# Last two chunks of a gated delta rule begin in rounds 1 and 2 instead of round 4, with the wait for one weight's split moved to their fourth step

## The reference

```python
# half 1: gated delta rule, 4 heads of 128, one scan forward and one backward
kk = einsum('bnhik,bnhjk->bnhij', k, k)
a_low = where(strict, kk * decay * beta[..., :, None], 0.0)
uw = triangular_solve(a_low + eye(C), rhs, left_side=True, lower=True, unit_diagonal=True)
def step(S, xs):                      # chunk after chunk
    v_new = u_i - einsum('bhck,bhkv->bhcv', w_i, S)
    o_i = einsum('bhck,bhkv->bhcv', q_i, S) + einsum('bhij,bhjv->bhiv', qk_i, v_new)
    S = S * gl_i[..., None, None] + einsum('bhck,bhcv->bhkv', k_i, v_new)
# half 2: attention with 8 query heads and 2 key heads of 64, rotated by row and column
o_at = axial_gqa_group(aq, ak, av, q_norm, k_norm)
mix = concatenate([o_dn, o_at], axis=-1) @ w_out
```

## Time and profile before

| | us |
|---|---|
| median of three runs | 1135.56 |
| the profiled execution's own time | 1134.65 |
| its span | 1132.9 |
| busy: PE / DVE / ACT / POOL | 1080.2 / 750.3 / 608.4 / 93.3 |
| delta stage on PE, first gates product to last `o` product | 799.14 to 915.85 |

### The profile page before, as it was taken

One profiled execution on the slowest core, in us unless ns is written; L12 is line 12 of the kernel. 1 busy time (PEld: TensorE's weight loads), 2 busy tenths in 40 slices (PEclk: granted clock), 3 DMA queues, 4 the chain that ended last, 5 costly groups with the idle time before them and its releaser, 6 DMA issues.

```text
span 1132.9 us, 19901 instructions
## 1 busy us (share of the span) xinstructions
PE 1080.2 (95%) x8119; PEld 959.5 (85%) x8119; DVE 750.3 (66%) x1254; ACT 608.4 (54%) x1098; POOL 93.3 (8%) x120
## 2 busy tenths in 40 slices
PE   6999998999999999999999999999679999999998
PEld 3989567989899899889899988999568878998986
DVE  1686887899997866567755447786575756444443
ACT  2544755554354556657445465547764536555453
POOL 0012671000000000000000000022420000000000
PEclk9999999999999999999999999999788999999999
DMA  9998116799998455433855652260000145555540
GB/s 371 408 400 339 39 38 260 269 347 370 347 354 301 149 186 187 144 135 144 339 195 187 229 177 106 75 259 2 1 2 21 40 153 200 186 186 186 186 149 38
DMA packets 33562, 218.27 MB, mean 193 GB/s; under 512 B 4528, under 2 KB 5296, under 8 KB 8896
## 3 DMA queue, kind: packets, MB, share of 16 engines
q1 hardware_dynamic: 33472, 217.00, 51.8%
HBM read 215.93 MB, written 1.05 MB: 192 GB/s over the span
## 4 chain that ended last, share of the span: by engine, by line
PE 79%; DVE 8%; ACT 7%; DMA 2%; issue 2%; POOL 1%; DVEq 0%; SPq 0%; ACTq 0%; POOLq 0%
PE bank L527 21%; PE bank L529 21%; PE bank L528 21%; ACT high L515 2%; DVE low L521 2%; DMA ring<-ada_halves 2%; PE bank L567 1%; PE bank L2485 1%; PE bank L644 1%; DVE y_tmp L1608 1%; PE bank L1150 1%; DVE stats L1610 1%; DVE y_tmp L1597 1%; PE bank L2774 1%; DMA ring<-raw_ksv 1%
## 5 line engine op out<-in xcount | busy, mean ns | idle before, releaser
L521 DVE TENSOR_TENSOR low<-ring,high 128x2048 fp32r<-128x2048 f32 (+1 forms) x139 | 317.4, 2286 | 234.9 <-ACT high L515 234.4
L515 ACT ACTIVATE high<-ring 128x2048 fp32r<-128x2048 f32 (+1 forms) x139 | 264.7, 1906 | 246.1 <-PE bank L529 171.0
L527 PE MATMUL bank<-act_high,high 128*128 128x256 f32 (+1 forms) x1072 | 308.5, 288 | 0.0
L529 PE MATMUL bank<-act_high,low 128*128 128x256 f32 (+1 forms) x1072 | 303.6, 283 | 0.0
L528 PE MATMUL bank<-act_low,high 128*128 128x256 f32 (+1 forms) x1072 | 303.5, 283 | 0.0
L527 PE MATMUL bank<-high,act_high 128*128 128x512 f32 (+1 forms) x632 | 233.3, 369 | 3.1 <-DVE act_low L3080 1.8
L529 PE MATMUL bank<-high,act_low 128*128 128x512 f32 (+1 forms) x632 | 230.8, 365 | 0.0
L528 PE MATMUL bank<-low,act_high 128*128 128x512 f32 (+1 forms) x632 | 230.6, 365 | 0.0
L527 PEld LDWEIGHTS bank<-act_high,high 128*128 128x128 f32 x1072 | 204.8, 191 | 4.7 <-issue 2.6
L528 PEld LDWEIGHTS bank<-act_low,high 128*128 128x128 f32 x1072 | 205.0, 191 | 2.4 <-issue 1.4
L529 PEld LDWEIGHTS bank<-act_high,low 128*128 128x128 f32 x1072 | 204.8, 191 | 0.0
(11 more groups left out here) (514 smaller groups left out, 1339.6 us busy)
## 6 DMA issues: line engine op xcount, KB each, us to landing
ring<-chunks SPq DMA_DIRECT2D x138, 1024.0 KB, 5.1
ring<-ada_halves SPq DMA_DIRECT2D x38, 1024.0 KB, 6.6
o_land<-ada_halves SPq DMA_DIRECT2D x6, 1024.0 KB, 11.4
ring<-raw_cmp SPq DMA_DIRECT2D x4, 1024.0 KB, 11.2
x_tok<-ada_halves SPq DMA_DIRECT2D x3, 1024.0 KB, 14.9
gate_rows<-ada_b SPq DMA_DIRECT2D x4, 512.0 KB, 9.7
bias<-bias_by_distance SPq DMA_DIRECT2D x1, 2048.0 KB, 12.9
ln_rows<-ln_g SPq DMA_DIRECT2D x4, 512.0 KB, 6.0
```

What stands on the lines that cost most here:

```text
L515: e.activation(weights(c)[0], in_ring(("w", c)), ACT.Copy).then_inc(*act.up("high", c))
L521: e.tensor_tensor(low, in_ring(("w", c)), high.bitcast(F32), ALU.subtract).then_inc(*vec.up("low", c))
L527: e.matmul(out_, ah, bh, start=start, stop=False)
L529: return e.matmul(out_, al, bh, start=False, stop=stop)
```

## The change

The last two chunks begin in rounds 1 and 2. What stood in their way is rearranged: `qdec` leaves the slots of OUT2 and OUT2+1 for a free place; the wait for the `low` of OUT2+1 goes from step 1 on PE to step 4 on DVE, and to the zeroing of `xT` on POOL, and step 1 waits for IN2+10 alone. Their scaled rows (`bv`, `bek`, which share a buffer with the meta chunk) are written one level later.

```diff
-                      **{... for i, n in enumerate(("x", "xT", "bek", "qdec"))},
+                      **{... for i, n in enumerate(("x", "xT", "bek"))},
                       "bv": mem.take(f"d{d}_bv_last", 4, P, at=after_cols + 8 * L2 + d * 512),
+                      "qdec": mem.take(f"d{d}_qdec_last", 4, P, at=(late_at + 6 * P + (2 * JOIN + 1) * HALF, after + 336 + D)[d]),
...
             elif not first:
-                e.wait_ge(*low_made(OUT2 + 1))
+                e.wait_ge(*low_made(IN2 + 10))
...
-            rows_level = 1 if first else 3
+            rows_level = 1 if first else 4
...
             e.wait_ge(*vec.at("a", k))
+            if real and not first:
+                e.wait_ge(*low_made(OUT2 + 1))
...
-        CHUNKS = (((0, 2), 0), ((1, 2), 0), ((0, 0), 0), ((1, 1), 0), ((0, 1), 4), ((1, 0), 4))
+        CHUNKS = (((0, 2), 0), ((1, 2), 0), ((0, 0), 0), ((1, 1), 0), ((0, 1), 1), ((1, 0), 2))
...
             e.wait_ge(*act.at("w", (d, t)))
+            if d != t:
+                e.wait_ge(*low_made(OUT2 + 1))
```

More of the change, by code:

```diff
@@ L2008, in program @@
         last_bufs = [{**{n: mem.take(f"d{d}_{n}_last", 4, P, at=early_at[d] + i * 512) for i, n in enumerate(("a", "aT", "w"))},
-                      **{n: mem.take(f"d{d}_{n}_last", 4, P, at=late_bufs[d] + i * 512) for i, n in enumerate(("x", "xT", "bek", "qdec"))},
+                      **{n: mem.take(f"d{d}_{n}_last", 4, P, at=late_bufs[d] + i * 512) for i, n in enumerate(("x", "xT", "bek"))},
                       "bv": mem.take(f"d{d}_bv_last", 4, P, at=after_cols + 8 * L2 + d * 512),
+                      "qdec": mem.take(f"d{d}_qdec_last", 4, P, at=(late_at + 6 * P + (2 * JOIN + 1) * HALF, after + 336 + D)[d]),
                       "qk": first_bufs[d]["qk_last"]} for d in range(2)]
```

## The result

The changed kernel takes 1137.81 us (median of 20 runs, 1132.62 to 1141.15), the kernel before beside it 1134.62 us (20 runs, 1130.49 to 1138.06). The ratio is 1.0024, with a 95% interval of 1.0013 to 1.0035: slower, by about 3 us. The profiled execution of the changed kernel, though, took 1133.5 us, less than the 1134.65 us of the one of before. It is one of the fastest of its twenty. That has to be explained first.

What follows compares the result with a forecast made beforehand. PE was taken as the bound, busy 95%, with 13.7 us idle from 804 to 850 us. The front's 3.1 us plus 1.65 us at the end made 4.8 us slower: 1139.8 us, range 1131 to 1146.

Steps and rivals of the forecast that it cites:

- the sum's main term: First part of the delta stage: round 8 ends 6.0 us late, minus 2.9 us of steps ahead, net 3.1 us late.
- the right ones: Signs: DVE round 3 at 820 to 822 us, ACT idle 6 us, logits 7 to 10 late, PE full, two holes.
- signs of being wrong: Logits before 836 us, PE idle under 13.7 us before it is full, or step 2 making ACT wait at no cost.
- the second rival: Delta stage: lateness equals the 2.9 us of steps ahead, only 1.65 us at the end remain; 1136.3 us, chance 0.17.
- The holes at the end: PE idle 0.75 us before the o product of (1, 0) and 0.9 us before the last values, together 1.65 us.
- The queue of DVE: Round 2: moved steps make DVE begin round 3 at about 821.1 us instead of 816.48, 4.6 us late.
- Round 3 on DVE: Its former 8.4 us, slow instruction included, plus 3.2 us of moved work, ending at 832.7 us.
- ACT's wait: ACT idle 6 us or more before the qdec exponential of (1, 0), behind DVE; first logits 8.9 us late.
- From the logits to the end of round 8: On PE, 19.9 us before the change shrink by 2.9 us of waits to 17.0 us; round 8 ends at 856.4.
- The clock: Rival: one more half-clock stretch on PE costs some 2.8 us, 1142.5 us, or one fewer, 1137.0; chance 0.15.
- The filled idle time: Rival: moved steps fill PE's idle time in the first part; -4.4 us, 1130.3 us, at most -6.7; chance 0.23.

Runs made afterwards that it cites:

- e5: Changed kernel plus 13 idle products, whose results nobody reads, in places where PE waits; ratio 0.9999 to the kernel before.
- e11: Kernel before plus 16 idle products in its two long PE waits; ratio 0.9976 to the kernel before.
- e9: Changed kernel with only (0, 1) early, in round 1, and (1, 0) in round 4 as before; 1130.2 us, ratio 0.9970 to the kernel before.
- e10: Changed kernel with only (1, 0) early, in round 2, and (0, 1) in round 4 as before; ratio 0.9995 to the kernel before.
- e4: Changed kernel with the last chunks' two step 2 exponentials written one round later on ACT; ratio 1.0003 to the kernel before.
- e2: Changed kernel without its new starting rounds, keeping the moved waits, new qdec place and later rows; ratio 0.9999 to the kernel before.
- e12: Kernel e9 plus 14 idle products in PE's waits; ratio 0.9953 to the kernel before, six executions.
- e3: Changed kernel plus 28 idle products at four places where PE waits in the first part; ratio 1.0032 to the kernel before.

## Why the prediction came out, and where its steps were wrong

The sign, the size (forecast 4.8 us by the sum, measured 3.2 us) and the range held. But the sum's main term was not what made the kernel slower, so that the number came out is in large part luck: a front that was to lose 3.1 us did not, and a clock that was given 0.15 cost about as much.

The prediction's own signs say so. Three of the right ones came (ACT idle for 6.69 us, PE full from 850 us on, two holes of 0.89 and 0.77 us at the end); DVE began round 3 just before its 820 us; the logits were 5.2 us late and not 7 to 10. And both signs of being wrong that have a number came: the logits at 835.73, before 836 us, and PE idle for 10.0 us from 804 to 850, less than 13.7. ACT reached the meta keys at 834.83, which was the condition of the second rival, *only the end counts*. Of the three it tells best what the profiled order does; the rest of the loss is the clock's.

- **The holes at the end**, 1.65 us forecast: 0.89 and 0.77 us in the profile. Right.
- **The queue of DVE.** Round 3 was to begin at 821.1 us and began at 819.94. The mechanism held, with one thing overlooked: six chunks are live in round 2, so the attention's step moves behind (1, 1), and its `K` product runs at 808.44 inside the wait for POOL instead of after it.
- **Round 3 on DVE**, 11.7 us forecast, took 9.3 (819.94 to 829.2). I took POOL's multiplication to be late by as much as DVE, so that it meets `x` of (1, 1) again. It began at 825.51, 4.2 us later than before, and `x` of (1, 1) at 824.42, only 3.3 us later; it met instructions that read a bank, and they took their usual 1.1 us. The multiplication for the last two chunks met `x` of (0, 1) instead (0.84 and 1.85 us in the DVE rows), where ACT was later anyway. The rule of the Trainium skill, "GPSIMD Engine Reference", section "Specifications", had been read rightly; these two durations agree with it.
- **ACT's wait** was forecast at 6 us or more and is 6.69. The logits were to be 8.9 us late and are 5.2 us late, by the two points above.
- **From the logits to the end of round 8** 17.0 us were forecast; it took 16.7 (835.73 to 852.4). Round 8 thus ends 2.0 us late, not 6.0, and with the same 2.9 us of steps ahead, which is my estimate and not measured, the front gains 0.9 us. This is the step that failed: the front was sized at 3.1 us lost, and is about 1 us gained in the profiled execution, although its clock there was the lower one.
- **The clock**, my third rival with 0.15. The runs point to it for the result: the changed kernel's median execution runs at 0.977 where that of before runs at 0.982, its executions at 0.983 take 5 to 6 us less than those around 0.975, and at equal clock it is not slower than before. e5 and e11 add only unread products, raise the clock and take off about 2.8 us each. I had counted one more or one fewer stretch as an accident of 2.8 us. It is the rule with this order, and not only after 850 us: even the fast profiled execution has 0.69 in the first part, where before has 0.78. By what the new order lowers the clock isn't shown.
- **The filled idle time**, the first rival (0.23), is what happens where only (0, 1) moves (e9). That it comes near the 1130.3 us of this rival is chance, since that figure was for both chunks. The figure also lies outside my range, which begins at 1131, although I wrote that the range holds a good half of this rival.

Not settled: why (1, 0) alone costs nothing (e10) while (0, 1) alone gains 4 us and both together lose 3. The clocks (0.981, 0.983, 0.977) go in the right direction but are half of it: at equal clock (0, 1) alone still gains 3.5 us, (1, 0) alone 0.8 and both together 0.7. Part of the difference between the halves is read from the waits: (0, 1) alone takes away the 2.9 us before the level-1 product of (1, 1), (1, 0) alone leaves it. So beside an early (0, 1) the early (1, 0) costs about 3 us by order and 3 more by the clock. The late queue behind ACT that the prediction followed is a likely cause of the first part; no run shows it by itself, and e4, which removes ACT's wait, brings back only 0.6 us at equal clock. Nor was it shown what decides in one execution, and not in the next, how long PE stands at half clock.

## What to carry to other kernels

Where engines run hand-written lists in step, ask of each moved piece not what it costs but what stands behind it on the engine that must wait: here two exponentials held up rows whose data were ready. Move one of two twins first: half of this change was worth 0.3%, the whole lost it and 0.2% more. And when the profiled execution goes against the median, look at the list of clocks before reading the trace, and compare kernels at equal clock.

## What was not expected of the hardware

- TensorE stood at its lower level (granted 0.50, that is 1.2 of 2.4 GHz) in windows in which it had no idle time at all: 865 to 870 us in e2, where most products were of 64 x 64. From 850 to 916 us such stretches add up to 7 us in the earlier trace rows, to 17 in the profile of e2, and to none in the profiled execution of the changed kernel. The twenty executions of this kernel differ by 8 us, and their times follow the mean clock (1132.6 us at 0.983, 1140.5 at 0.975); the stretches with PE full are only one of the places where the half clock lies (see e10).
- Idle products in waits of 1 to 4.5 us came with a mean granted clock higher by 0.002 to 0.008 (e12, e11, e5) and took 0.2% off the kernel before (e11). Where they lasted longer than the wait they cost time: ten of them took 4.61 us behind a late bank, and the logits came 3.4 us later (e3).
- A VectorE instruction with two inputs in SBUF took 1.85 us beside POOL's multiplication and 0.84 us without it (L2653); those of the same stretch that read a bank took 1.08 us for four of 128 x 128 (L2645, e.g. at 826.13), as elsewhere.
